# A three-block transformer kernel: the experts' gate and up projections as three products of split operands

## What is computed

```
def hier_moe(xn, w_group, b_group, w_expert, b_expert, w_gate, w_up, w_down):
    ...
    e_w, e_idx = lax.top_k(e_prob, TOPK_IN_GROUP)
    ...
    hid = silu(einsum('td,edf->tef', xt, w_gate)) * einsum('td,edf->tef', xt, w_up)
    y = einsum('tef,efd->td', hid * cw[:, :, None], w_down)
```

## Times and profile before

| | us |
|---|---|
| median of 3 runs | 1228.33 |
| lowest and highest | 1228.23, 1233.76 |
| the profiled execution's own time | 1233.52 |
| span in its trace (first to last instruction) | 1231.7 |
| TensorE busy | 1123.2 (91%) |
| DVE busy | 601.6 (49%) |
| ACT busy | 537.0 (44%) |
| mean granted TensorE clock | 0.950 |

### The profile page before, as it was taken

The page is one execution under the profiler, slowest core; times in us unless marked ns, Lnnn a source line. Parts: engine busy times, 40 slices in busy tenths (PEclk is TensorE's granted clock), DMA queues, the critical chain, the costliest instruction groups (busy, mean ns, idle before and its releaser), DMA issues.

```text
span 1231.7 us, 15828 instructions
## 1 busy us (share of the span) xinstructions
PE 1123.2 (91%) x5580; PEld 911.6 (74%) x5580; DVE 601.6 (49%) x1177; ACT 537.0 (44%) x1020; POOL 72.1 (6%) x111
## 2 busy tenths in 40 slices
PE   5958889999998997899899999978979899999977
PEld 4857677999997885797677777756867687777756
DVE  4536675666666564555523223256645532232344
ACT  4435564444444532584433332245566443322234
POOL 8000600000000020000100000000000100000000
PEclk8988699999999998999999999979989999999989
DMA  9683013666654543003658888513501948888700
GB/s 293 174 216 133 1 35 120 205 189 186 188 169 166 168 152 137 1 2 137 256 202 297 303 304 286 178 53 119 170 1 38 353 142 300 297 307 290 237 0 35
DMA packets 105075, 210.68 MB, mean 171 GB/s; under 512 B 7992, under 2 KB 49816, under 8 KB 104752
## 3 DMA queue, kind: packets, MB, share of 16 engines
q1 hardware_dynamic: 101984, 204.04, 48.7%
q0 software_dynamic: 2736, 4.80, 2.1%
q10 hardware_dynamic: 288, 0.99, 0.2%
HBM read 207.17 MB, written 2.62 MB: 170 GB/s over the span
## 4 chain that ended last, share of the span: by engine, by line
PE 83%; DVE 7%; ACT 5%; issue 3%; DMA 2%; SPq 1%; ACTq 0%; DVEq 0%
PE bank L787 21%; PE bank L1448 20%; PE bank L1465 10%; PE bank L1179 8%; PE bank L1189 7%; PE bank L882 3%; PE bank L706 2%; PE bank L863 2%; PE bank L1490 2%; PE bank L871 2%; PE bank L1907 1%; ACT x_high L760 1%; DMA ring<-in_w_uq 1%; PE bank L1335 1%; PE bank L862 1%
## 5 line engine op out<-in xcount | busy, mean ns | idle before, releaser
L787 PE MATMUL bank<-weight_parts,x_high 128*128 128x512 f32 (+3 forms) x832 | 248.8, 384 | 27.3 <-issue 13.8
L1448 PE MATMUL bank<-expert_w,block_x 128*128 128x256 f32 x1120 | 260.6, 379 | 1.0 <-ACT block_x L1414 1.0
L1448 PEld LDWEIGHTS bank<-expert_w,block_x 128*128 128x128 f32 x1120 | 207.3, 190 | 59.9 <-issue 33.0
L787 PEld LDWEIGHTS bank<-weight_parts,x_high 128*128 128x128 f32 x832 | 157.1, 196 | 58.3 <-issue 20.3
L808 DVE TENSOR_TENSOR weight_parts<-ring,weight_parts 128x1024 fp32r<-128x1024 f32 (+3 forms) x108 | 121.2, 1141 | 91.4 <-ACT weight_parts L805 91.2
L787 PE MATMUL bank<-weight_parts,x_low 128*128 128x512 f32 (+3 forms) x416 | 158.8, 382 | 0.0
L805 ACT CAST weight_parts<-ring 128x1024 fp32r<-128x1024 f32 (+3 forms) x108 | 103.8, 982 | 118.6 <-PE bank L787 91.5
L1465 PE MATMUL bank<-expert_w,junk 128*128 128x512 f32 x280 | 131.7, 593 | 0.8 <-issue 0.8
L1516 DVE SCALAR_TENSOR_TENSOR arena<-bank,home_w,arena 128x1024 f32 x64 | 82.2, 1284 | 79.4 <-PE bank L1465 79.4
L1503 DVE TENSOR_TENSOR junk<-junk,bank 128x128 f32<-128x128 f32 x70 | 20.2, 288 | 176.0 <-ACT junk L1427 176.0
L1179 PE MATMUL bank<-x_high,parts 128*128 128x256 f32 x512 | 98.5, 285 | 0.6 <-DVE parts L1243 0.6
(11 more groups left out here) (320 smaller groups left out, 1430.5 us busy)
## 6 DMA issues: line engine op xcount, KB each, us to landing
expert_w<-in_moe_w_gate SPq DMA_DIRECT2D x70, 512.0 KB, 5.2
expert_w<-in_moe_w_up SPq DMA_DIRECT2D x70, 512.0 KB, 6.1
expert_w<-in_moe_w_down SPq DMA_DIRECT2D x70, 512.0 KB, 4.2
ring<-in_w_ff SPq DMA_DIRECT2D x64, 512.0 KB, 3.9
ring<-in_w_in SPq DMA_DIRECT2D x16, 512.0 KB, 11.1
ring<-in_a_w_in SPq DMA_DIRECT2D x16, 512.0 KB, 4.6
ring<-in_ple_w_gate SPq DMA_DIRECT2D x16, 512.0 KB, 5.0
ring<-in_w_o SPq DMA_DIRECT2D x8, 512.0 KB, 6.4
```

The costliest lines, as they stand in the source:

```text
L787: mm = nc.tensor.matmul(bank[:, j["m"] % 4, 0:n], j["operand"][x][:, 2 * c + kk, at[0]:at[1]], weight_parts[:, number % PAIRS, w, kk * n:( ...
L1448: mm = nc.tensor.matmul(bank[:, 4 + b % 2, 0:256].rearrange("p (q n) -> p q n", q=2), block_x[:, b % 2, k, :], w[:, k], start=k == 0, stop ...
```

## The change

Gate and up are computed as high x high, high x low and low x high of fp32r parts, 24 products a block for 8.

- ACT casts gate and up of a block to `expert_high` (two buffers) in two pieces of 1024 columns, each piece 4 of the 8 chunks of both matrices; DVE writes the low part over the f32 weights in their slot (`expert_low`). Both are done two blocks ahead.
- `sorted_x` becomes `sorted_high`; DVE makes `sorted_low` from PSUM, 8 more instructions, and the second half of the gather now waits for these. ACT copies high slots to `block_high`, DVE low slots to `block_low`.
- Tile numbers are read eight at a time (`tiles_of`), on ACT and on DVE.
- On TensorE gate/up is no longer halved around the transpose; the order is gate/up of b, transpose of b-1, down product of b-2. DVE's add follows three blocks behind.
- `DEPTH` goes from 7 to 5.
- The second part of the route's computation on DVE (`dve_masks`: `cw`, `home_w`, `extra_w`) moves behind the first splits, the sort and the first low copies.
- The combine takes tile 0 of `acc` as it is, as f32 products, and splits only tiles 1 to 3.
- Several tiles move in memory (`ple_y`, `place_turned`).

The core of the diff:

```
-BLOCKS, DEPTH = EXPERTS + EXTRA, 7
+BLOCKS, DEPTH = EXPERTS + EXTRA, 5
...
-                    pe.wait_ge(sorted_ready, KB * layer + k - 3)
+                    pe.wait_ge(sorted_split, KB * layer + k - 3)
...
+    def dve_sort(dve, layer):
+
+        for k in range(KB):
+            dve.wait_ge(sorted_ready, KB * layer + k + 1)
+            nc.vector.scalar_tensor_tensor(out=sorted_low[:, k, :], in0=bank[:, 4 + k % 4, :],
+                                           scalar=gains[f"ln_ffn{layer}"][:, k:k + 1], in1=sorted_high[:, k, :],
+                                           op0=ALU.mult, op1=ALU.subtract).then_inc(sorted_split, 1)
...
+    def half_of(w, j):
+        return w.rearrange("p (q k n) -> p q k n", q=2, k=KB)[:, :, 4 * j:4 * j + 4, :]
+
+    def act_cast_expert(act, layer, b):
+
+        act.wait_ge(*up_at(layer, b))
+        if b >= 2:
+            act.wait_ge(ex_up, BLOCKS * layer + b - 1)
+        for j in range(2):
+            nc.scalar.copy(half_of(expert_high[:, b % 2, :], j),
+                           half_of(expert_w[:, b % DEPTH, 0:2048], j)).then_inc(ex_cast, 1)
+
+    def dve_split_expert(dve, layer, b, halves=(0, 1)):
+
+        for j in halves:
+            dve.wait_ge(ex_cast, 2 * (BLOCKS * layer + b) + j + 1)
+            nc.vector.tensor_tensor(half_of(expert_low[:, b % DEPTH, 0:2048], j),
+                                    half_of(expert_w[:, b % DEPTH, 0:2048], j),
+                                    half_of(expert_high[:, b % 2, :], j), ALU.subtract).then_inc(ex_split, 1)
...
         for b in range(BLOCKS):
             act.wait_ge(ex_up, first + b + 1)
             nc.scalar.activation(silus[:, b % 2, :], bank[:, 4 + b % 2, 0:P], ACT.Silu).then_inc(ex_silu, 1)
+            if b:
+                keep(b - 1)
             if b + 2 < BLOCKS:
-                act_block_x(act, layer, b + 2)
...
+                act_cast_expert(act, layer, b + 2)
+                copy_x(b + 2)
...
+            for k in range(KB):
+                if k % 4 == 0:
+                    pe.wait_ge(ex_split, 2 * (first + b) + k // 4 + 1)
+                for n, (x, w) in enumerate(((block_high, high), (block_high, low), (block_low, high))):
+                    mm = nc.tensor.matmul(bank[:, 4 + b % 2, 0:256].rearrange("p (q n) -> p q n", q=2),
+                                          x[:, b % 2, k, :], w[:, k], start=k == 0 and n == 0,
+                                          stop=k == KB - 1 and n == 2)
...
-        for b in range(BLOCKS):
-            gate_up(b, 0, 4)
-            if b:
+        for b in range(BLOCKS + 2):
+            if b < BLOCKS:
+                gate_up(b)
+            if 1 <= b <= BLOCKS:
                 turn_hid(b - 1)
...
+            if b >= 2:
+                low(b - 2)
...
+        pe.wait_ge(ex_added, BLOCKS * (layer + 1))
+        for t in range(TILES):
+            for half in range(2):
+                nc.tensor.matmul(bank[:, 2 * t + half, :], place_turned[:, 0, t * P:(t + 1) * P].bitcast(F32),
+                                 acc[:, half * 512:(half + 1) * 512], start=True, stop=False)
+        for q in range(1, SORT_TILES):
+            pe.wait_ge(acc_split, (SORT_TILES - 1) * layer + q)
...
         for b in range(BLOCKS):
             hid(b)
-            if b:
-                add(b - 1)
...
+            if b + 2 < BLOCKS:
+                copy_x(b + 2)
+            if b >= 3:
+                add(b - 3)
+            if b + 2 < BLOCKS:
+                dve_split_expert(dve, layer, b + 2)
```

More of the change, by code:

```diff
@@ L1418, in act_experts, with copy_x @@
         act.wait_ge(steps_ready, layer + 1)
-        act_block_x(act, layer, 0)
-        act_block_x(act, layer, 1)
+        tiles = []
+        def copy_x(b):
+            if b < EXPERTS and b % 8 == 0:
+                tiles.extend(tiles_of(act, b))
+            at = tiles[b] * P if b < EXPERTS else (b - EXPERTS + 1) * P
+            nc.scalar.copy(block_high[:, b % 2], sorted_high[:, :, ds(at, P)]).then_inc(ex_copied, 1)
+        act.wait_ge(sorted_ready, KB * (layer + 1))
+        copy_x(0)
+        copy_x(1)
         act.wait_ge(place_flipped, layer + 1)
@@ L1424, in act_experts, with keep @@
                            bank[:, half, :]).then_inc(place_kept, 1)
+        def keep(b):
+            act.wait_ge(ex_turned, first + b + 1)
+            nc.scalar.copy(hidTs[:, b % 2, :], bank[:, 6 + b % 2, 0:P]).then_inc(ex_kept, 1)
         for b in range(BLOCKS):
@@ L1438, in pe_experts, with gate_up @@
         first = BLOCKS * layer
-        def gate_up(b, lo, hi):
-            if lo == 0:
-                pe.wait_ge(*up_at(layer, b))
-                pe.wait_ge(ex_copied, first + b + 1)
-                if b >= 2:
-                    pe.wait_ge(ex_hid, first + b - 1)
-            w = expert_w[:, b % DEPTH, 0:2048].rearrange("p (q k n) -> p k q n", q=2, k=KB)
-            for k in range(lo, hi):
-                mm = nc.tensor.matmul(bank[:, 4 + b % 2, 0:256].rearrange("p (q n) -> p q n", q=2), block_x[:, b % 2, k, :],
-                                      w[:, k], start=k == 0, stop=k == KB - 1)
-            if hi == KB:
-                mm.then_inc(ex_up, 1)
+        def gate_up(b):
+            pe.wait_ge(ex_copied, first + b + 1)
+            pe.wait_ge(ex_copied_low, first + b + 1)
+            if b >= 2:
+                pe.wait_ge(ex_hid, first + b - 1)
+            high, low = (w.rearrange("p (q k n) -> p k q n", q=2, k=KB)
+                         for w in (expert_high[:, b % 2, :], expert_low[:, b % DEPTH, 0:2048]))
+            for k in range(KB):
[5 more added lines that the diff above has]
+                                          stop=k == KB - 1 and n == 2)
+            mm.then_inc(ex_up, 1)
         def turn_hid(b):
@@ L1490, in pe_combine @@
                         mm = nc.tensor.matmul(bank[:, 2 * t + half, :], place_turned[:, q, t * P:(t + 1) * P],
-                                              x[:, q, half * 512:(half + 1) * 512], start=q == 0 and x is acc_high,
+                                              x[:, q, half * 512:(half + 1) * 512], start=False,
                                               stop=q == SORT_TILES - 1 and x is acc_low)
@@ L1517, in add, with copy_x @@
                                    scalar=share_of, in1=here, op0=ALU.mult, op1=ALU.add).then_inc(ex_added, 1)
+        tiles = []
+        def copy_x(b):
+            if b < EXPERTS and b % 8 == 0:
+                tiles.extend(tiles_of(dve, b))
+            at = tiles[b] * P if b < EXPERTS else (b - EXPERTS + 1) * P
+            if b >= 2:
+                dve.wait_ge(ex_up, first + b - 1)
+            v.tensor_copy(block_low[:, b % 2], sorted_low[:, :, ds(at, P)]).then_inc(ex_copied_low, 1)
+        dve.wait_ge(sorted_split, KB * (layer + 1))
+        copy_x(0)
+        copy_x(1)
+        dve_split_expert(dve, layer, 1)
+        dve_masks(dve, layer)
         dve.wait_ge(acc_zeroed, layer + 1)
@@ L1585, in dve_route @@
         dve.wait_ge(chosen_made, layer + 1)
+        dve_split_expert(dve, layer, 0, (0,))
         dve.wait_ge(slots_made, layer + 1)
```

122 lines of the change are left out of this document (68 added, 54 removed).

## The result

| | kernel before | changed kernel |
|---|---|---|
| median, seven runs each, us | 1228.33 (1227.09 to 1236.37) | 1221.20 (1218.46 to 1226.32) |
| profiled execution, us (its span) | 1233.52 (1231.7) | 1219.45 (1217.7) |
| ratio of the two kernels' times | | 0.9912, 95% interval 0.9886 to 0.9938 |

The change makes the kernel 0.9% faster. The forecast was 1205, 1.9% faster; 1221.2 lies inside its range, but less than half of the forecast gain came by the ratio, and by the two profiled executions 14.1 of the 23.4 us. The 30 runs of the kernel before that stood beside experiments 1 to 10 fall into two groups, 7 at 1227.1 to 1228.6 with a mean granted clock of 0.957 and 23 at 1231.6 to 1236.2 with 0.947 to 0.954; the median above is from the first group, the profiled run from the second, and which one a run falls into isn't explained here.

What follows compares the result with a forecast made beforehand. TensorE alone was taken to set the pace. Per layer +12.0 opening, -20.2 stage, -3.5 combine make -11.7, two layers -23.4: profiled 1233.5 becomes 1210.1, median 1205, range 1195 to 1232.

Steps and rivals of the forecast that it cites:

- The block: Expert stage: TensorE needs 4.70 us a block, with 24 products in 2.87 us; pace taken as 4.72.
- rival 5: Gate/up products no faster with the split pattern, 0.144 us instead of 0.120, pace 5.28, 1241 us; chance 0.05.
- DVE's side: DVE's work per expert block: low copy 0.70 us, sum 4.71 by durations or 4.4 by spacing, about level with TensorE.
- rival 2: DVE's low copy runs at the two-operand rate, 1.22 us: 1231 with overlap, chance 0.12; 1250 without, chance 0.07.
- Rival 1: Expert stage: DVE becomes the bound mildly, durations not overlapping, pace 4.9, 1217 us; chance 0.15.
- The opening: Start of each expert stage: later cw and half clock delay gate/up by 12.0 us a layer, bounds +9 to +14.
- The stage: Expert stage from first gate/up to its end: 165.5 us against 185.75, -20.2 us a layer.
- A read of tile numbers is absorbed: Steady expert blocks: a read of eight, taken as 1.3 us, is absorbed; the add comes 2 us early.
- The transfers: Expert weight loads with five slots: needed some 11 us after issue, landing in 4.5 to 7.2 us, so hidden.
- Rival 4: Expert weights come late: landing at 13.5 us makes the pace 5.28 and the time 1241 us; chance 0.03.
- The combine: After the expert stage: tile 0 as f32, then split products; -3.5 us a layer, bounds -2 and -3.9.
- Rival 3: Opening costs more: clock stays low into gate/up and DVE reaches cw later, +18 a layer, 1217 us; chance 0.06.

Runs made afterwards that it cites:

- experiment 1: Changed kernel with the operations that make cw moved between the two halves of DVE's sort; median 1206.11 us, ratio to the kernel before 0.979.
- experiment 2: Changed kernel with tile numbers read without range checks on ACT and DVE; one execution, 1211.66 us.
- experiment 3: Changed kernel with no tile numbers read, every expert using tile 0; one execution, 1215.08 us.
- experiment 4: Changed kernel with 88 spare transposes keeping TensorE busy between the gather and the shares; span 1214.8 us.
- experiment 5: Changed kernel with gate and up of the next block queued ahead of the low slots; 1219.05 us, span 1217.3.
- experiment 6: Kernel before with only the changed kernel's combine; median 1226.69 us, ratio to the kernel before 0.995.
- experiment 7: Kernel before with five weight slots in place of seven, nothing else; 1233.92 us, span 1232.1.
- experiment 8: Changed kernel with cw and first tile-number read between sort halves, no range checks, gate/up queued one block sooner; 1195.46 us, ratio to the kernel before 0.969.
- experiment 9: Experiment 8 with the loads queued as in the changed kernel; median 1195.09 us, ratio to the kernel before 0.971.
- experiment 10: Experiment 8 with the masks moved behind the splits of expert 2; median 1190.54 us, ratio to the kernel before 0.966.

## Why the prediction was half right

**The block: right.** TensorE 4.70 forecast, 4.69 measured; 24 products in 2.87 us, so the split pattern costs nothing (rival 5 falls). The forecast's 4.72 a block was right for 29 of the 32 and wrong for the three with a read.

**DVE's side: right.** The copy was put at 0.70 and lasts 0.69; rival 2 falls. The Trainium skill (VectorE: DVE Perf Modes, The perf-mode tier table) gives fp32 copies within SBUF twice the rate of two-tensor operations, 0.70 us here as an estimate. The row, 0.69, agrees, also for an fp32r source in runs of 128 elements. Rival 1, DVE as a mild bound, falls as well: DVE waits for ACT in each plain block. That the operations overlap a little shows in pairs of subtractions, 2.35 us for two of 1.22.

**The opening: the term was too small.** +12.0 was forecast, +14.4 and +14.1 came. The step that failed is the read of eight tile numbers, 1.3 us with an upper bound of 1.8; it measured 3.3 in the first layer and 3.0 in the second. I had taken it from ACT's stand in front of a single number and doubled that for eight, as if a read were one price and not a load and eight checked steps. What else stands in front of cw was a little cheaper than forecast (2.72 for four sort instructions), so cw was done 1.8 us late, at 628.2 in place of 626.4. Shares and transposes at half clock took 5.4 us in place of 4.9, and gate/up started at 633.67, against 631.3. That the half clock would reach into the first gate/up, the sum had nothing for.

**The stage: right in its pace, wrong at four places.** 165.5 us were forecast; 169.6 and 168.2 came. "A read of tile numbers is absorbed" failed, and by the same term. The slack of 2 us in front of the add was right: a read of 2.7 us costs TensorE 0.8, one of 3.05 costs 1.16, and both times 1.9 are absorbed. But the slack was set against a read of 1.3 us. The longer one goes through the copy and the add to TensorE, 1.16, 1.09 and 0.82 us in the first layer and 2.4 together in the second. The first gate/up at half clock adds 1.55 and 0.73. The third adds 0.26 at full clock, since its first product starts behind an idle time (a gate/up behind one takes 3.10 to 3.13 us in experiments 9 and 10 too). In experiment 2 the stage lasted 166.4 us with its cold start, which is the forecast and the clock.

**The transfers: right in effect, though not in margin.** Nothing was to be felt below a landing of 11 us. Landings reached 8.8, and ACT, whose casts come ahead of TensorE's use, waited 10.4 us. Hardly any of it is TensorE time: 0.27 us of one block went with the waits in experiment 5, in experiment 9 they are back without a late block, and experiment 7 shows five slots to be enough at the old pace. Put at nothing, the term was small but not nothing. Rival 4 falls.

**The combine: right.** -3.5 forecast, -3.4 measured, -3.6 alone in experiment 6.

**Sum.** Per layer +14.4 and +14.1, -16.1 and -17.6, -3.4 and -3.4: -12.1 together, against -23.4. Of the 11.3 missing, 4.5 are the opening and 6.7 the stage. What lies outside ran 1.9 us shorter in that execution: 2.9 less between the two layers, where one linear took 22.03 us with the clock at 1.00 in place of 23.67 at 0.93, and 1.0 more behind the second layer, where the last linear took 23.40 in place of 22.28. So the profiled execution came to 1219.45 where 1210.1 was forecast. Rival 3 named the mechanism, a clock that stays low into gate/up and a late cw; at +14.3 the opening lies between the forecast's +12 and its +18, nearer the forecast. (The prediction's chances, as listed, add up to 0.12 for no change and 0.15 for slower, not 0.13 and 0.14.)

**The median.** A second step failed. I took the 5.2 us by which the profiled run of before lay above the median off the changed kernel's forecast as well. But of the two groups of runs named with the result the median of before lay in one and the profiled run in the other, where most runs are. The changed kernel's seven runs lie at 1218.5 to 1226.3, with clocks of 0.937 to 0.946. The forecast for its median should have stayed near 1210. By the two medians the gain is 7.1 us; by the ratio, 0.88%, it is 10.8; and the traces' 14.1 holds for two executions of like clock in front of the stage.

## What to carry to other kernels

When a change puts work into an engine's queue, follow what stands behind it there for another engine: seven small operations for TensorE, stuck behind sorts, splits and a read, cost more than the change's measured gain, and moving them was a small edit. Price a read of several registers per value, checks included; at a high load such a stall reaches the bound through whoever waits in the same queue. A long wait in the list costs nothing until a block of the bounding engine is shown to be late by it, so measure the spacing of the blocks first.

## What the runs showed of the hardware

- A read of eight integers into DVE's registers with range checks stands 2.5 to 3.1 us in DVE's queue inside a stage, mostly 2.7 (0.33 for the load, some 0.27 for each value, the rest around them), and 3.31 and 3.00 at the openings, where the load alone is 0.85 in the first layer. Without the checks it is 0.5 to 0.8 inside a stage, and 1.04 and 0.78 at the openings.
- The granted clock after an idle time isn't the same in every execution. In experiments 8 and 9 TensorE did the same and then idled 1.50 us at the same place. The granted clock was 0.65 over the 24 products behind it in the one, which took 4.42 us, and 1.00 in the other, where they took 3.10. Why isn't explained here:

```profile
632.25 4.42 PE bank L1519 x24
```

```profile
626.01 3.10 PE bank L1508 x24
```

- The same holds in the busy linears: the last one, 90 products, lasts 22.3 us in seven of the twelve traces, 23.2 to 23.5 in four (the changed kernel's, 23.40, and those of experiments 1 to 3) and 22.03 in one. The span of a single execution tells no more than some 5 us here, while a stretch counted from a marker inside the trace repeats to 0.1 us, unless the clock falls in it.
